# The opening of a one-core block program: order of the first roundings, two transfers for the first weights, and zero products on TensorE

## The chip, the cores and the metric

The program runs on one core of one Trainium2 chip, in one launch. The metric is the device time of that core in microseconds (us). The core has TensorE (PE in the profile; its weight loads are PEld), VectorE (DVE), ScalarE (ACT), GpSimd (POOL) and SyncE (SP), which here issues all the transfers, and 16 DMA engines that carry them.

## The reference, cut to what matters

The reference is two transformer blocks of two layers each over a sequence of 256 tokens and a width of 1024, in float32. The change touches only the first layer of the first block, up to its first few projections:

```python
def rmsnorm(x, g):
    xf = x.astype(jnp.float32)
    y = xf * lax.rsqrt(jnp.mean(xf * xf, axis=-1, keepdims=True) + RMS_EPS)
    return (y * g.astype(jnp.float32)).astype(x.dtype)

for l in range(DEPTH):
    h = rmsnorm(x, attn_norm[l])
    proj = h @ w_in[l]
    ...     # latent attention, gated convolution, pooling, windowed attention, output product
    x = x + mixed @ w_o[l]
    gate, up = jnp.split(rmsnorm(x, ffn_norm[l]) @ w_gate_up[l], 2, axis=-1)
    x = x + (jax.nn.silu(gate) * up) @ w_down[l]
```

The second block (state-space, recurrent and linear-attention mixers, and 32 experts per layer) follows and is not touched.

## The kernel before, in words

The activations x lie transposed in the core's memory: 128 partitions by 8 feature tiles by 256 tokens. The 16 output tiles of the first projection (1952 columns, 2048 with the repeated rotary ones) are computed one after another by `project(n)`. To keep float32 accuracy with the faster rounded format, every operand is split into a rounded high part and the rest: x times the norm's gain is rounded by ScalarE (`PreNorm.round`, L582) and the rest taken by VectorE (`PreNorm.rest`, L605); a weight tile is rounded by ScalarE (`Ring.round`, L505) and its rest taken by VectorE (`Ring.rest`, L511). `one_tile` then issues three products for each of 8 feature tiles, 24 per output tile (L630 to L632). The factor 1/rms is not in x: it is applied when a pair of projections leaves the accumulators (`evacuate`, L767), so the sum of squares can come later than the first products. ScalarE squares x in 8 instructions (`PreNorm.square`, L587), TensorE sums them over the partitions with a matrix of ones (`PreNorm.sum`, L613), and ScalarE makes 1/rms (`PreNorm.scale`, L593 and L596).

The weights of the first block come through a ring: `Ring.raw` has 4 slots, each with a unit of two weight tiles (1 MB); `high` and `low` have 4 places of one tile each. Four semaphore chains order it: SP issues the load of a unit into a slot once both tiles that were in it are split; ScalarE rounds tile n once its unit is loaded and tile n-4 has been used by TensorE; VectorE takes the rest after that; TensorE waits for the rest.

Nothing schedules the work at run time or when the program is built. Each engine has its own instruction stream in the order in which the functions for it are written in `stage_mix1`, and runs it strictly in that order; so a waiting instruction holds up all that stand behind it on its engine. In the first layer these are, before the change:

- SP (`load_first`): gains, x in two halves, unit 0, the matrix of ones, units 1 to 3, constants, the small weights of the attention (L720 to L722), then units 4 and on, each behind its slot's split.
- ScalarE: 8 tiles of x, weight tiles 0 to 3, 8 squares, 1/rms, weight tiles 4 to 8, then ln and exp for the latent norms (L956 to L961), weight tiles 9 and 10.
- VectorE: constants (`set_constants`, with a zeroed bank of 128x512 bfloat16 at L560), the rests of x, of weight tiles 0 to 4, pair 0 out, 5, 6, pair 1 out, and so on; behind the rest of weight tile 8 the scaling of the latent vectors (L840).
- TensorE: `project(0)`, the sum of squares, `project(1)` to `project(4)`, sums for the latent norms, `project(5)`, `project(6)`, then the query product (L1104), which waits for the scaled latent vectors.

`psX` is the last of the eight accumulator banks; the sum of squares goes there too, later.

Of the kernel before, what the change touches and what calls it, by code (L numbers as in the profile page):

```python
# [26 lines left out]
P = 128  # L27
D = 1024
S = 256
DT = D // P  # L30
# [288 lines left out]
class Stream:  # L319
# [28 lines left out]
    def round(self, act, i):  # L348

        act.wait_ge(self.loaded[i % self.slots], 16 * (i // self.slots + 1))  # L350
        if i >= self.n2:

            act.wait_ge(self.used, i - self.n2 + 1)
        for a, b in self.halves(i):
            act.activation(self.high[:, i % self.n2, a:b], self.raw[:, i % self.slots, a:b], ACT.Copy)\
                .then_inc(self.rounded, 1)

    def rest(self, dve, i):

        for n, (a, b) in enumerate(self.halves(i)):  # L360
            dve.wait_ge(self.rounded, 2 * i + n + 1)
            dve.tensor_tensor(self.low[:, i % self.n2, a:b], self.raw[:, i % self.slots, a:b],
                              self.high[:, i % self.n2, a:b], ALU.subtract).then_inc(self.split, 1)
# [83 lines left out]
W_HALF = DT * P  # L447
# [4 lines left out]
G_ORDER1 = (3, 2, 0, 1)  # L452
AHEAD = 4
LATE = 2


def ffn_order():
# [9 lines left out]
class Ring(Stage):  # L467
# [4 lines left out]
    def __init__(self, nc, dram):  # L472
        super().__init__(nc, "ring")
        self.dram = dram
        self.raw = self.sb("raw", [P, self.SLOTS, W_UNIT])
        self.high = self.sb("high", [P, AHEAD, W_HALF], F32R)
        self.low = self.sb("low", [P, AHEAD, W_HALF], F32R)
        self.loaded = [self.sem(f"loaded{i}") for i in range(self.SLOTS)]
        self.rounded = self.sem("rounded")
        self.split = self.sem("split")  # L480
        self.used = self.sem("used")
        self.issued = 0

    def load_while_split(self, sp, splits, most=N_ALL1):

        while 2 * self.issued < N_ALL1 and self.issued < most and \
# [4 lines left out]
            sp.dma_start(self.raw[:, g % self.SLOTS], self.dram[g]).then_inc(self.loaded[g % self.SLOTS], 16)  # L491
            self.issued += 1

    def raw_half(self, n):
        return self.raw[:, (n // 2) % self.SLOTS, (n % 2) * W_HALF:(n % 2 + 1) * W_HALF]

    def round(self, act, n):
        if n >= N_ALL1:
            return
        if n % 2 == 0:  # L500
            act.wait_ge(self.loaded[(n // 2) % self.SLOTS], 16 * (n // 2 // self.SLOTS + 1))
        if n >= AHEAD:

            act.wait_ge(self.used, n - AHEAD + 1)
        act.activation(self.high[:, n % AHEAD], self.raw_half(n), ACT.Copy).then_inc(self.rounded, 1)  # L505
# [33 lines left out]
def load_first(sp, k, f, ring, a):  # L539

    x = a["x_t"].rearrange("p (t s) -> p t s", t=DT)
    half = DT // 2
    sp.dma_start(f.vecs[:], a["vec1"].rearrange("l p n -> p l n")).then_inc(f.vec_loaded, 16)
    for i in range(2):
        sp.dma_start(k.x[:, half * i:half * (i + 1)], x[:, half * i:half * (i + 1)]).then_inc(f.x_loaded[i], 16)
    ring.load_while_split(sp, 0, 1)
    early = 2 * P
    sp.dma_start(k.const[:, 0:early], a["const"][:, 0:early]).then_inc(f.ones_loaded, 16)
    ring.load_while_split(sp, 0)
    sp.dma_start(f.const1[:], a["const"][:, N_KEPT:]).then_inc(f.const_loaded, 16)  # L550
    sp.dma_start(k.const[:, early:], a["const"][:, early:N_KEPT]).then_inc(f.const_loaded, 16)
    sp.dma_start(k.fin_g[:], a["fin_g"]).then_inc(k.gains_loaded, 16)
    sp.dma_start(k.ln[:], a["ln2"].rearrange("l p n -> p l n")).then_inc(k.gains_loaded, 16)
# [9 lines left out]
class PreNorm:  # L563
# [9 lines left out]
        self.ln_done = st.sem("ln_done")  # L573
        self.rstd_ready = st.sem("rstd_ready")

    def round(self, act):
        if self.first:
            act.wait_ge(self.f.vec_loaded, 16)
        for t in range(DT):
            if self.first and t % (DT // 2) == 0:  # L580
                act.wait_ge(self.f.x_loaded[t // (DT // 2)], 16)
            act.activation(self.f.high[:, t], self.k.x[:, t], ACT.Copy, scale=self.gain[:, t:t + 1])\  # L582
                .then_inc(self.rounded, 1)
# [11 lines left out]
        act.wait_ge(self.ln_done, 1)  # L595
        act.activation(self.f.rstd[:], self.f.lnv[:], ACT.Exp, scale=-0.5).then_inc(self.rstd_ready, 1)  # L596

    def rest(self, dve):
        if self.first:
            dve.wait_ge(self.f.vec_loaded, 16)  # L600
        for t in range(DT):
            if self.first and t % (DT // 2) == 0:
                dve.wait_ge(self.f.x_loaded[t // (DT // 2)], 16)
            dve.wait_ge(self.rounded, t + 1)
            dve.scalar_tensor_tensor(self.f.low[:, t], self.k.x[:, t], self.gain[:, t:t + 1], self.f.high[:, t],  # L605
                                     ALU.mult, ALU.subtract).then_inc(self.split, 1)
# [48 lines left out]
def stage_mix1(nc, k, f, ring, zero, L, a):  # L655
# [3 lines left out]
    with Stage(nc, f"mix{L}") as st:  # L659
        base = L * N_LAYER1  # L660
        first = L == 0
# [32 lines left out]
        norm = PreNorm(k, st, f, vecs[:, V1["attn_norm"][0]:], ps[:, 7], first)  # L694
# [12 lines left out]
        psX = ps[:, 7]  # L707
# [6 lines left out]
        with nc.Block() as block:  # L714

            @block.sync
            def _(sp):
# [4 lines left out]
                sp.dma_start(poolw[:], a["pool_w"][L].rearrange("p (k c) -> p k c", k=2)).then_inc(w_loaded, 16)  # L722
                ring.load_while_split(sp, base + N_MIX1 + AHEAD - LATE)

# [34 lines left out]
            def _(dve):  # L759
# [55 lines left out]

                if first:
                    set_constants(dve, k)
                norm.rest(dve)
                for n in range(0 if first else AHEAD - LATE, AHEAD):
                    ring.rest(dve, base + n)  # L820
                ring.rest(dve, base + 4)
                evacuate(0)
# [61 lines left out]
                group(3)  # L884
                for n in range(22, 28 - LATE):
                    ring.rest(dve, base + n)
# [9 lines left out]
            def _(act):  # L896
# [43 lines left out]

                if first:
                    act.preload_act_table_set("natural_log_exp_and_others")
                norm.round(act)
                if first:
                    for n in range(AHEAD):
                        ring.round(act, n)
                else:
                    act.preload_act_table_set("natural_log_exp_and_others")
                norm.square(act)
                if not first:  # L950
                    ring.round(act, base + AHEAD - 1)
                norm.scale(act)
                for n in range(4, 9):
# [54 lines left out]
            def _(pe):  # L1008
                def project(n):
                    ring.ready(pe, base + n)  # L1010
                    if n % 2 == 0 and n >= 4:

                        pe.wait_ge(evac, n // 2 - 1)
                    one_tile(pe, ps[:, (n // 2) % 2, (n % 2) * S:(n % 2 + 1) * S], ring.tiles(base + n), f,
                             norm.split if n == 0 else None).then_inc(ring.used, 1)
# [59 lines left out]
                def output(j):  # L1075
# [10 lines left out]
                            ins.then_inc(out_done, 1)  # L1086
                    ins.then_inc(ring.used, 1)

                project(0)
                norm.sum(pe)  # L1090
                for n in range(1, 5):
                    project(n)
                pe.wait_ge(latent_sq, 1)
                pe.wait_ge(norm.ln_done, 1)
# [14 lines left out]
                for blk in range(SB):  # L1109
                    ins = pe.matmul(ps[:, 6, blk * S:(blk + 1) * S], cn[:, 2, blk * P:(blk + 1) * P], wukv[:, 1],  # L1110
                                    start=True, stop=True)
# [23 lines left out]
                for g in range(4):  # L1135
                    rows, t = slice(64 * (g % 2), 64 * (g % 2) + 64), g // 2
# [25 lines left out]
def stage_ffn1(nc, k, f, ring, zero, L):  # L1162
# [3 lines left out]
    with Stage(nc, f"ffn{L}") as st:  # L1166
# [14 lines left out]
        with nc.Block() as block:  # L1181

            @block.sync
            def _(sp):
                ring.load_while_split(sp, base + len(order) + AHEAD - LATE)

            @block.vector
            def _(dve):
                ch = Chain(dve, dve_step)
                norm.rest(dve)  # L1190
                for n in range(AHEAD - LATE, AHEAD):
                    ring.rest(dve, base + n)
# [1980 lines left out]
```

## Time and profile before

| | us |
|---|---|
| runs before: median of 3 (lowest, highest) | 1953.72 (1951.14, 1955.69) |
| the profiled execution, its own time | 1956.74 |
| its span in the trace | 1955.0 |
| TensorE busy in the span | 1858.0 |
| VectorE, ScalarE busy | 832.1, 637.3 |
| granted TensorE clock, mean | 0.996 |

The span runs from the first to the last recorded instruction. "Busy" counts an engine's instructions, with the ends of matmuls modelled; the start-to-start distance of two matmuls tells more than their length. In a row of the timeline a group of like instructions is merged as "x8", and the bracket says how long the engine stood idle before it and which instruction or transfer released it. The granted clock is TensorE's as a share of full speed.

### The profile page before, as it was taken

Reading aid. Unit: us, or ns where it says so; the run is one execution under the profiler, and the core shown is the slowest. Engines: PE = TensorE matmul, PEld = TensorE weight load, DVE = VectorE, ACT = ScalarE, POOL = GpSimd, SP = SyncE. Lnnn points to the kernel's source line nnn. Section 1 sums busy time; section 2 is a strip of 40 time slices with the busy share of each in tenths; the row PEclk is TensorE's granted clock in tenths of the full one; section 3 lists DMA queues with packets and bytes.
Section 4 is the critical chain, followed back from the end, with each engine's and each line's share of the span. In section 5 each row is a group of like instructions: output and inputs, shape, how many; then the busy total and the mean of one; then the engine's idle time right before and its main releaser. Section 6 shows DMA issues by size and latency. Waiting matters only on the chain. (4 is left out here: it accounts for less than half of the span.)

```text
span 1955.0 us, 35987 instructions
## 1 busy us (share of the span) xinstructions
PE 1858.0 (95%) x15616; PEld 1266.6 (65%) x15626; DVE 832.1 (43%) x1687; ACT 637.3 (33%) x1209; POOL 52.2 (3%) x58
## 2 busy tenths in 40 slices
PE   7999999899999998899999999989899999999997
PEld 6889998789997887644444434378775444444443
DVE  5767777767775576411111111155734111111113
ACT  4565555565555342311111111143313111111112
POOL 0500000400000000000000000000000000000000
PEclk9999999999999999999999999999999999999999
DMA  7245554235552338499999999743395999999993
GB/s 287 96 147 191 192 194 169 87 131 193 191 176 70 98 99 342 177 407 426 427 427 427 427 427 426 309 124 110 127 380 192 428 427 427 426 426 427 427 426 164
DMA packets 54529, 540.18 MB, mean 276 GB/s; under 512 B 8640, under 2 KB 9568, under 8 KB 16736
## 3 DMA queue, kind: packets, MB, share of 16 engines
q1 hardware_dynamic: 54368, 537.83, 68.6%
q8 instruction: 126, 2.06, 0.4%
q14 instruction: 35, 0.29, 0.0%
HBM read 536.76 MB, written 1.05 MB: 275 GB/s over the span
## 5 line engine op out<-in xcount | busy, mean ns | idle before, releaser
L2971 PE MATMUL experts_psG<-places_gu,experts_xc 128*64 128x512 f32 x1344 | 297.8, 593 | 9.3 <-DMA places_gu<-in_moe_up 9.3
L511 DVE TENSOR_TENSOR ring_low<-ring_raw,ring_high 128x1024 fp32r<-128x1024 f32 x180 | 222.4, 1246 | 100.6 <-ACT ring_high L505 100.5
L2971 PEld LDWEIGHTS experts_psG<-places_gu,experts_xc 128*64 128x64 f32 x1344 | 96.8, 137 | 203.1 <-issue 184.3
L644 PE MATMUL ffn_ps<-first_x_split,ring_high 128*128 128x512 f32 x616 | 220.6, 396 | 0.3
L2898 DVE SCALAR_TENSOR_TENSOR experts_yc_low<-experts_psD,experts_slot_gate,experts_yc_high 128x512 fp32r<-128x512 f32 x64 | 48.1, 751 | 388.5 <-ACT experts_yc_high L2934 388.5
L505 ACT ACTIVATE ring_high<-ring_raw 128x1024 fp32r<-128x1024 f32 x180 | 186.8, 1051 | 70.5 <-PE ffn_ps L646 30.7
L645 PE MATMUL ffn_ps<-first_x_split,ring_low 128*128 128x256 f32 x704 | 183.4, 281 | 0.0
L2888 DVE TENSOR_TENSOR experts_sig<-experts_sig,experts_psG 128x256 f32<-128x256 f32 x64 | 27.0, 421 | 356.3 <-ACT experts_sig L2922 356.3
L2971 PE MATMUL experts_psG<-weights_gu,experts_xc 128*64 128x512 f32 x704 | 156.2, 593 | 5.1 <-DMA weights_gu<-in_moe_up 3.7
L2922 ACT ACTIVATE experts_sig<-experts_psG 128x256 f32<-128x256 f32 x64 | 24.6, 384 | 411.3 <-PE experts_psG L2971 411.3
L645 PEld LDWEIGHTS ffn_ps<-first_x_split,ring_low 128*128 128x128 f32 x704 | 132.1, 188 | 7.1
L644 PEld LDWEIGHTS ffn_ps<-first_x_split,ring_high 128*128 128x128 f32 x616 | 115.8, 188 | 24.9 <-issue 1.2
L2934 ACT ACTIVATE experts_yc_high<-experts_psD,experts_slot_gate 128x512 fp32r<-128x512 f32 x64 | 44.0, 687 | 262.9 <-PE experts_psD L3001 262.9
L2971 PEld LDWEIGHTS experts_psG<-weights_gu,experts_xc 128*64 128x64 f32 x704 | 50.0, 137 | 106.4 <-issue 95.0
L3001 PE MATMUL experts_psD<-places_d,experts_hT 128*64 128x512 f32 x512 | 116.9, 598 | 0.0
L2947 PE MATMUL experts_psX<-parts_selb,parts_x 128*128 128x64 bf16 x3072 | 99.8, 193 | 0.0
L622 PE MATMUL ffn_ps<-ffn_act_high,ring_low 128*128 128x256 f32 x352 | 98.6, 280 | 0.0
L621 PE MATMUL ffn_ps<-ffn_act_low,ring_high 128*128 128x256 f32 x352 | 98.3, 279 | 0.0
L620 PE MATMUL ffn_ps<-ffn_act_high,ring_high 128*128 128x256 f32 x352 | 98.3, 279 | 0.0
L2947 PEld LDWEIGHTS experts_psX<-parts_selb,parts_x 128*128 128x128 bf16 x3072 | 93.6, 98 | 0.5
L2001 PE MATMUL mixers_ps<-x_resid,mixers_w_raw 128*128 128x256 f32 x384 | 88.3, 386 | 4.5 <-ACT x_resid L233 2.2
L630 PE MATMUL mix_ps<-first_x_split,ring_high 128*128 128x256 f32 x256 | 76.6, 299 | 14.1 <-DVE ring_low L511 11.9
(531 smaller groups left out, 3243.4 us busy)
## 6 DMA issues: line engine op xcount, KB each, us to landing
ring_raw<-in_w SPq DMA_DIRECT2D x90, 1024.0 KB, 4.9
places_gu<-in_moe_gate SPq DMA_DIRECT2D x42, 2048.0 KB, 28.1
places_gu<-in_moe_up SPq DMA_DIRECT2D x42, 2048.0 KB, 29.6
places_d<-in_moe_down SPq DMA_DIRECT2D x32, 2048.0 KB, 26.0
weights_gu<-in_moe_up SPq DMA_DIRECT2D x22, 2048.0 KB, 28.0
weights_gu<-in_moe_gate SPq DMA_DIRECT2D x20, 2048.0 KB, 28.7
weights_d<-in_moe_down SPq DMA_DIRECT2D x16, 2048.0 KB, 26.0
experts_d_more<-in_moe_down SPq DMA_DIRECT2D x16, 2048.0 KB, 27.8
```

Source lines behind the costliest of these rows:

```text
L505: act.activation(self.high[:, n % AHEAD], self.raw_half(n), ACT.Copy).then_inc(self.rounded, 1)
L511: dve.tensor_tensor(self.low[:, n % AHEAD], self.raw_half(n), self.high[:, n % AHEAD], ALU.subtract)\
L620: pe.matmul(out, w[0][:, kk], high, start=False, stop=False)
L621: pe.matmul(out, w[0][:, kk], low, start=False, stop=False)
L622: return pe.matmul(out, w[1][:, kk], high, start=False, stop=stop)
L630: pe.matmul(out, w[0][:, kk], f.high[:, kk], start=kk == 0, stop=False)
L644: pe.matmul(out, w[0][:, kk], f.both[:, :, kk], start=kk == 0, stop=False)
L645: ins = pe.matmul(out[:, 0], w[1][:, kk], f.high[:, kk], start=False, stop=False)
L2001: return pe.matmul(out, a, c, start=kc == 0, stop=kc == DT - 1)
L2947: ins = pe.matmul(psX[:, t * SLOTS:(t + 1) * SLOTS], m.parts[:, i, blk, t * P:(t + 1) * P], selb[:, par, blk, 0:SLOTS], start=i == 0 and b ...
L2971: ins = pe.matmul(out, xc[:, kk], wgu[gu[0]][:, kk, :, j * S:(j + 1) * S], start=kk == 0, stop=kk == DT - 1)
L3001: ins = pe.matmul(psD[rows, :], hT[:, c, j * SLOTS:(j + 1) * SLOTS], wd[d[0]][:, 2 * j + c, i * 512:(i + 1) * 512], start=j == 0 and c == ...
```

## The change

SP now loads the first unit in two transfers of 512 KB, one per weight tile, and the first has a semaphore of its own. ScalarE rounds weight tile 0 between tiles 3 and 4 of x, and squares x right behind weight tile 1, ahead of weight tiles 2 and 3. VectorE takes the rests in the same order. TensorE first multiplies the zeroed bank by itself 24 times into `psX`, as soon as VectorE has set it, and sums the squares behind `project(1)`, where it stood behind `project(0)`. All of it is for the first layer alone; the other layers keep their order.

```diff
+ZEROS = 24
...
+    def load_first(self, sp):
+
+        for n, sem in enumerate((self.first_loaded, self.loaded[0])):
+            sp.dma_start(self.raw_half(n), self.dram[0, :, n * W_HALF:(n + 1) * W_HALF]).then_inc(sem, 16)
+        self.issued = 1
...
     def round(self, act, n):
         if n >= N_ALL1:
             return
-        if n % 2 == 0:
+        if n == 0:
+            act.wait_ge(self.first_loaded, 16)
+        elif n % 2 == 0 or n == 1:
             act.wait_ge(self.loaded[(n // 2) % self.SLOTS], 16 * (n // 2 // self.SLOTS + 1))
...
-    ring.load_while_split(sp, 0, 1)
+    ring.load_first(sp)
...
-    def round(self, act):
+    def round(self, act, tiles=range(DT)):
...
-        for t in range(DT):
+        for t in tiles:
...
-    def rest(self, dve):
+    def rest(self, dve, tiles=range(DT)):
...
-                norm.rest(dve)
-                for n in range(0 if first else AHEAD - LATE, AHEAD):
+                if first:
+                    norm.rest(dve, range(0, DT // 2))
+                    ring.rest(dve, 0)
+                    norm.rest(dve, range(DT // 2, DT))
+                    ring.rest(dve, 1)
+                else:
+                    norm.rest(dve)
+                for n in range(AHEAD - LATE, AHEAD):
                     ring.rest(dve, base + n)
...
-                norm.round(act)
                 if first:
-                    for n in range(AHEAD):
-                        ring.round(act, n)
+                    norm.round(act, range(0, DT // 2))
+                    ring.round(act, 0)
+                    norm.round(act, range(DT // 2, DT))
+                    ring.round(act, 1)
+                    norm.square(act)
+                    ring.round(act, 2)
+                    ring.round(act, 3)
                 else:
+                    norm.round(act)
                     act.preload_act_table_set("natural_log_exp_and_others")
-                norm.square(act)
-                if not first:
+                    norm.square(act)
                     ring.round(act, base + AHEAD - 1)
...
+                if first:
+                    pe.wait_ge(k.constants_set, 7)
+                    for _ in range(ZEROS):
+                        pe.matmul(psX, k.zero[:, 0:P], k.zero[:], start=True, stop=True)
                 project(0)
-                norm.sum(pe)
-                for n in range(1, 5):
+                if first:
+                    project(1)
+                    norm.sum(pe)
+                else:
+                    norm.sum(pe)
+                    project(1)
+                for n in range(2, 5):
                     project(n)
```

ScalarE, at the start of the first layer, before the change (`first_x_split` is the high part of x, `ring_high` that of a weight tile, `first_sq` the squares; `ring_loaded0` and `ring_loaded1` are the loads of units 0 and 1):

```order
L942 ACT_TABLE_LOAD
L582 ACTIVATE first_x_split<-x_resid,first_vecs 128x256 [waits first_x_loaded0,first_vec_loaded]
L582 ACTIVATE first_x_split<-x_resid,first_vecs 128x256 x3
L582 ACTIVATE first_x_split<-x_resid,first_vecs 128x256 [waits first_x_loaded1]
L582 ACTIVATE first_x_split<-x_resid,first_vecs 128x256 x3
L505 ACTIVATE ring_high<-ring_raw 128x1024 [waits ring_loaded0]
L505 ACTIVATE ring_high<-ring_raw 128x1024
L505 ACTIVATE ring_high<-ring_raw 128x1024 [waits ring_loaded1]
L505 ACTIVATE ring_high<-ring_raw 128x1024
L587 ACTIVATE first_sq<-x_resid 128x256 x8
```

The same engine and place after it (L582, L505 and L587 have become L592, L515 and L597):

```order
L958 ACT_TABLE_LOAD
L592 ACTIVATE first_x_split<-x_resid,first_vecs 128x256 [waits first_x_loaded0,first_vec_loaded]
L592 ACTIVATE first_x_split<-x_resid,first_vecs 128x256 x3
L515 ACTIVATE ring_high<-ring_raw 128x1024 [waits ring_first_loaded]
L592 ACTIVATE first_x_split<-x_resid,first_vecs 128x256 [waits first_x_loaded1,first_vec_loaded]
L592 ACTIVATE first_x_split<-x_resid,first_vecs 128x256 x3
L515 ACTIVATE ring_high<-ring_raw 128x1024 [waits ring_loaded0]
L597 ACTIVATE first_sq<-x_resid 128x256 x8
L515 ACTIVATE ring_high<-ring_raw 128x1024 [waits ring_loaded1]
L515 ACTIVATE ring_high<-ring_raw 128x1024
```

Weight tile 0 has moved ahead of four tiles of x and waits for its own half of unit 0; the squares have moved ahead of weight tiles 2 and 3.

TensorE, the first instructions of the first layer after the change; before it the stream began with the L640 row (then L630):

```order
L1112 MATMUL mix_ps<-zero_bank 128x512 [waits constants_set]
L1112 MATMUL mix_ps<-zero_bank 128x512 x23
L640 MATMUL mix_ps<-first_x_split,ring_high 128x256 [waits mix0_x_split,ring_split]
L641 MATMUL mix_ps<-first_x_split,ring_high 128x256
L642 MATMUL mix_ps<-first_x_split,ring_low 128x256
```

The 24 zero products stand ahead of `project(0)` and wait for the constants alone.

## Rows read from the trace of the kernel before

**Rows 1.** The page: span, and busy time of each engine.

```profile
span 1955.0 us, 35987 instructions
PE 1858.0 (95%) x15616; PEld 1266.6 (65%) x15626; DVE 832.1 (43%) x1687; ACT 637.3 (33%) x1209; POOL 52.2 (3%) x58
```

**Rows 2.** Windows: stretch, length, busy PE, PEld, DVE, ACT, POOL, clock, DMA share, GB/s.

```profile
0.00:50.00 50.00, 37.32 (x256) 34.72 (x258) 27.99 (x41) 24.35 (x38) 0.52 (x9) 1.00 0.73 281
900.00:950.00 50.00, 50.00 (x456) 23.14 (x454) 8.05 (x28) 9.14 (x24) 0.00 (x0) 1.00 1.01 426
```

**Rows 3.** PE's waits over the span: us in total, times, longest.

```profile
PE mix_ps L630 <- DVE ring_low L511: 11.9, 1, 11.9
PE experts_psG L2971 <- DMA places_gu<-in_moe_up: 9.3, 10, 1.9
```

**Rows 4.** Timeline of ACT: start, length, instruction, idle before and releaser.

```profile
5.64 3.30 ACT L582 ACTIVATE first_x_split<-x_resid,first_vecs 128x256 fp32r<-128x256 f32 x8 [3.65 <-DMA x_resid<-in_x_t]
9.53 2.00 ACT L505 ACTIVATE ring_high<-ring_raw 128x1024 fp32r<-128x1024 f32 x2 [0.59 <-DMA ring_raw<-in_w]
...
14.51 2.55 ACT L587 ACTIVATE first_sq<-x_resid 128x256 f32<-128x256 f32 x8
...
31.86 1.06 ACT L505 ACTIVATE ring_high<-ring_raw 128x1024 fp32r<-128x1024 f32 x1 [1.82 <-PE mix_ps L632]
33.09 0.47 ACT L956 ACTIVATE mix_g_lnv<-mix_ps,eps_sb 128x256 f32<-128x256 f32 x1 [0.18 <-PE mix_ps L1097]
```

**Rows 5.** Timeline of DVE.

```profile
1.00 0.27 DVE L560 MEMSET zero_bank<- 128x256 uint32 x1
6.29 3.25 DVE L605 SCALAR_TENSOR_TENSOR first_x_split<-x_resid,first_vecs,first_x_split 128x256 fp32r<-128x256 f32 x8 [5.02 <-ACT first_x_split L582]
10.61 2.36 DVE L511 TENSOR_TENSOR ring_low<-ring_raw,ring_high 128x1024 fp32r<-128x1024 f32 x2 [1.06 <-ACT ring_high L505]
...
35.12 1.27 DVE L840 SCALAR_TENSOR_TENSOR mix_cn<-mix_proj,first_vecs,mix_g_rstd 128x256 f32<-128x256 f32 x3
```

**Rows 6.** Timeline of PE.

```profile
11.89 0.58 PE L630 MATMUL mix_ps<-first_x_split,ring_high 128*128 128x256 f32 x1 [11.89 <-DVE ring_low L511]
...
16.48 0.28 PE L630 MATMUL mix_ps<-first_x_split,ring_high 128*128 128x256 f32 x1
...
16.84 3.61 PE L613 MATMUL mix_ps<-first_sq,const 128*128 128x256 f32 x16
20.10 0.47 PE L630 MATMUL mix_ps<-first_x_split,ring_high 128*128 128x256 f32 x1
...
23.12 0.28 PE L630 MATMUL mix_ps<-first_x_split,ring_high 128*128 128x256 f32 x1
...
38.54 3.62 PE L1104 MATMUL mix_ps<-mix_cn,mix_wuq 128*128 128x256 f32 x16
```

**Rows 7.** Timeline of SP's queue, stretches 0:60 and 14:14.7.

```profile
1.22 0.93 SPq L545 DMA_DIRECT2D x_resid<-in_x_t  x2
...
14.60 2.10 SPq L491 DMA_DIRECT2D ring_raw<-in_w  x1
```

**Rows 8.** DMA issues, stretches 2:3 and 14:15: KB, us to landing.

```profile
x_resid<-in_x_t SPq DMA_DIRECT2D x1, 512.0 KB, 5.2
...
ring_raw<-in_w SPq DMA_DIRECT2D x1, 1024.0 KB, 15.2
```

**Rows 9.** Windows round three long pauses of PE, columns as in rows 2.

```profile
308.90:311.30 2.40, 0.20 (x3) 0.08 (x1) 1.54 (x4) 1.23 (x4) 0.33 (x5) 1.00 0.61 227
...
619.00:621.40 2.40, 0.17 (x1) 0.03 (x1) 1.17 (x3) 1.54 (x4) 0.00 (x0) 1.00 0.00 0
...
1283.00:1285.00 2.00, 0.00 (x0) 0.00 (x0) 1.13 (x3) 1.34 (x4) 0.00 (x0) 1.00 0.01 4
...
1286.00:1288.00 2.00, 2.00 (x7) 1.58 (x6) 1.17 (x5) 1.98 (x6) 0.00 (x0) 0.54 0.00 0
```

**Rows 10.** Line 652, zero products of a later stage: count, shortest/median/longest ns, first and last start.

```profile
L652 PE MATMUL ffn_ps<-zero_bank x3: 377/378/378, 118.6 to 119.0; 128*128 128x512 bf16 x3
```

More of the change, by code:

```diff
@@ L478, in __init__ @@
         self.loaded = [self.sem(f"loaded{i}") for i in range(self.SLOTS)]
+        self.first_loaded = self.sem("first_loaded")
         self.rounded = self.sem("rounded")
@@ L596, in scale @@
         act.activation(self.f.rstd[:], self.f.lnv[:], ACT.Exp, scale=-0.5).then_inc(self.rstd_ready, 1)
-    def rest(self, dve):
+    def rest(self, dve, tiles=range(DT)):
         if self.first:
             dve.wait_ge(self.f.vec_loaded, 16)
-        for t in range(DT):
+        for t in tiles:
             if self.first and t % (DT // 2) == 0:
```

## The prediction

> **What bounds the kernel now.** I read the page first: TensorE is busy for 1858.0 of 1955.0 us [rows 1]. Then the windows: there are two kinds of stretch, the opening, in which TensorE is busy 37.3 of 50 us, and the expert stretches, in which the DMA engines run at 426 GB/s and TensorE is hardly ever idle [rows 2]. Then TensorE's waits: the largest single one of the whole program, 11.9 us, is its first, which ends with VectorE's rest of weight tile 0; the waits for expert weights are 9.3 us in ten pieces [rows 3]. So the program begins with a chain of transfers and roundings, and from 11.89 us on TensorE's queue sets the time. I then read the three timelines of the first 40 us side by side [rows 4 to 6].
>
> The opening chain before: x lands, ScalarE rounds its 8 tiles from 5.64 to 8.94, waits 0.59 us for unit 0 and rounds weight tile 0 from 9.53 on [rows 4]; VectorE takes its rest from 10.61 to about 11.83 (two rests of 1.22 in 2.36 us, [rows 5]); TensorE starts at 11.89 [rows 6]. Its first 21 products then take until 16.48, 0.22 us each, against 0.12 behind it: between the first products of tile 1 and tile 2 lie 24 products in 3.02 us, of which 0.19 is the change over from the sum [rows 6]. The granted clock column says 1.00 there, but the pace is that of the lower of the clock's two levels (256 columns in 0.213 us is 1.2 GHz; 0.107 would be 2.4). So project(0) lost 4.95 - 2.9 = about 2.05 us to a clock that rose only after 4.6 us of work behind an engine that had been idle from the start.
>
> **The change, part by part.**
>
> First transfer and new order of the roundings. The second half of x is issued at about 1.7 us (two issues in 0.93 from 1.22, [rows 7]) and lands 5.2 us later, at 6.9 [rows 8]; unit 0, twice its size, is there at 9.53 [rows 4]. The halves of unit 0 share these 2.6 us: the first lands half-way, at 8.2. I take 8.2; the ends are 8.0 and 8.6 (if the two halves' packets mix a good deal). ScalarE is free at 5.64 + 4 x 0.40 = 7.3, so it now waits 0.9 us for weights that come 1.3 us earlier. It rounds tile 0 from 8.2 to 9.25 (the pair of L505 takes 2.00 us, so 1.05 for one and 0.95 from start to start). VectorE takes the rest from 9.28 to 10.5, and TensorE can start at 10.57, **1.32 us earlier**.
>
> Will the rest of x be in time? ScalarE rounds tiles 4 to 7 from 9.15, one every 0.40, until 10.85; VectorE takes their rests behind the weights' rest, from 10.45, one every 0.40 (8 in 3.25 us, [rows 5]), so they are ready at 10.9, 11.3, 11.7 and 12.1. TensorE at full pace wants tile 4 at 10.57 + 4 x 0.36 = 12.0. No wait.
>
> Weight tile 1: ScalarE 10.75 to 11.8 (its half has landed at 9.5), VectorE 12.0 to 13.25, usable at 13.3. At full pace project(0) ends at 10.57 + 2.90 = 13.47. It fits by 0.15 us; an error here costs no more than itself.
>
> Zero products. VectorE has the zeroed bank at 1.27 [rows 5], so TensorE starts them at 1.33. Their pace in this trace, warm, is 0.21 us (length 0.378 us, three between 118.6 and 119.0, [rows 10]: 512 columns at 2.4 GHz); no row shows them at the lower level, for which I double it, 0.43. If the clock rises as it did before, 4.6 us after the first product, then 10.8 of the 24 are done at 5.9 us, and the other 13.2 take 2.8 us: the burst ends at 8.75. At the lower level throughout it would end at 1.33 + 24 x 0.427 = 11.6. The burst is hidden as long as it ends before 10.57. Behind it is a **new pause of 1.8 us** (8.75 to 10.57). What do such pauses do to the clock here? Three of 2.2 us are in the trace: behind those that end at 311.25 and 621.40 it stays at 1.00, behind the one that ends at 1285 it falls, to 0.54 from 1286 on [rows 9]. A shorter pause than all three, with dense work on both sides: I take it that the clock holds, about three times in four.
>
> The Trainium skill bears on this ("TensorE: Matmul & The Clock Gate", section "What's actually happening"): the default state is throttled, activity releases it, and the clock gate looks at how busy the array has been, not at what it multiplies. By that rule zeros serve as well as data; the trace of before agrees on the idle start and the slow first products, and has no burst of zeros long enough to show the rest. The sum by the rule is the one below. The same page lets the clock fall only after an idle window; the fall at 1286 follows a pause no longer than two that were harmless, so the rows, not the rule, set my one in four.
>
> With the clock up, project(0) takes 2.90 us in place of 4.95: the first product costs some 0.07 more and 24 x 0.118 = 2.83. **2.05 us gained.**
>
> Squares and their sum. project(1) runs 13.47 to 16.30. ScalarE squares from 11.7 to 14.3 (2.55 us, [rows 4]), and TensorE sums from 16.30, without a wait, 3.26 us (16.84 to 20.10, [rows 6]), to 19.56. The move itself saves nothing on TensorE; it keeps the sum from standing before squares that would not be ready (before, they ended at 17.06). Rounding tiles 2 and 3 now stands behind the squares: ScalarE 14.3 to 16.3, VectorE 15.3 to 17.9; tile 2 is ready at 16.6 and wanted at 19.75. Hidden. 1/rms comes at 20.8, tile 4 is rounded 20.7 to 21.8 and split at 23.0, wanted at 19.56 + 0.19 + 2 x 2.83 = 25.4. Hidden.
>
> So tile 2 starts at 19.56 + 0.19 = 19.75 where tile 2 stood at 23.12: **3.37 us in all** (1.32 + 2.05).
>
> Is it given back? The next landing that ScalarE meets is unit 4 (tiles 8 and 9): issued at 14.60 [rows 7], landed 15.2 us later, at 29.8 [rows 8], because all that SP issued before it goes first. Before, tile 8 was rounded at 31.86, released by TensorE; 3.37 earlier is 28.5. So there is a **new wait of 1.3 us on ScalarE**, up to 1.75 if the additional issue (0.43 us) shows in the landing. Queued behind it is the ln of the latent norms (before at 33.09, [rows 4]), which now starts at 30.8 to 31.25 and not at 29.7, and on VectorE the rest of tile 8 and the scaled latent vectors. These ended at 35.12 + 1.27 = 36.39 [rows 5]; I get 33.6 to 34.1. The query product that takes them started at 38.54 [rows 6], now 35.17. Slack 1.1 to 1.6 us, where there were 2.15. Hidden, at no cost. Later waits all hang on chains that move with TensorE, and the expert loads too are issued when buffers come free, not at a fixed time: the 3.4 us should reach the end.
>
> **The sum.** Against the profiled execution's own time: 1956.74 - 3.4 = 1953.3 us. That execution lies 3.0 us above the median of the runs, for no reason in the trace, so I give the forecast on the median's scale: 1953.72 - 3.4 = 1950.3 us. From above: if the half lands at 8.6, 0.4 less; if the clock rises late in other executions of before, up to about 0.6 more.
>
> **The rivals.**
>
> The clock falls in the pause, or in the first product's microseconds. For: the fall at 1286 [rows 9]; before, it stayed low for the first 4.6 us. Against: two of three pauses. Then project(0) loses up to 2.05 again, and at the latest starts as computed at 10.57: the gain is 1.3 to 1.7 us, 1952.2 us.
>
> Zeros do not raise the clock. No row here shows that they do. Then the burst ends at 11.6, project(0) starts at 11.65 at the low level and gains 0.25 us: 1953.5 us.
>
> The burst becomes the bound: **slower**. No row shows a long row of such products at the low level, each with its own weight load. If zeros do not raise the clock, and a weight load lay beside its product and not under the one before, a product would take 0.43 + 0.21 = 0.64 us and the burst 15.4 us. project(0) would start at 16.7, still at the low level, take its 4.95 us, and tile 2 would start at 16.7 + 4.95 + 2.83 + 3.26 + 0.19 = 27.9 against 23.12: 4.8 us slower, 1958.5 us. The point from which it decides is a mean zero product of (11.89 - 1.33) / 24 = 0.44 us with the clock low. Against: between 20.10 and 23.12 in rows 6 the weight loads lie under the products (24 in 3.02 us, 0.12 each behind the first), and 0.427 is just short of 0.44.
>
> The gain is given back at unit 4: for it the slack of 1.1 us must go, which takes a landing after about 31 us; a landing at 32 would cost 1 us, leaving 1951.3.
>
> **How the numbers follow.** Forecast 0.62; clock falls 0.20; zeros do not count 0.07; burst the bound 0.04; given back at unit 4, 0.07. The median of three runs that lie 4.5 us apart is itself uncertain by some 1.5 us, and this holds for both kernels, so a measured difference strays by about 2 us around each case. A difference of less than 0.2% (3.9 us) can't be told from none here. The forecast's 3.4 lies just inside it: of its 0.62, 0.28 falls beyond 3.9; the other gaining cases give 0.03 more, and 0.04 for falls of the clock at other pauses, whose place against the clock's own rhythm is shifted (each costs or spares some 1.7 us). Faster 0.35, same 0.59, slower 0.06. The range: 1950.3 with 3.4 to either side, taking in the falling clock and the zeros that don't count: 1946.8 to 1954.0. The forecast's own is 1947.8 to 1952.6.
>
> **What would show it.** L1112 x24 from 1.33 to about 8.8 with its pace halving on the way; L515 for tile 0 at 8.2; the first L640 at 10.6 and its pace 0.12 from the second product on; the sum (L623) at 16.3, the second project pair from 19.75; ScalarE waiting 1.3 us for a transfer at about 28.5; the query product at 35.2 without a wait. Wrong would be: products at 0.21 us after 10.6, a burst that ends after 10.6, or a query product released by VectorE.

## The result, and the profile after

The changed kernel takes 1963.26 us (median of 10 runs, 1957.69 to 1967.65), the kernel before, beside it, 1956.86 (10 runs, 1951.14 to 1958.91): a ratio of 1.0036, 95% interval 1.0023 to 1.0048. It is 6.4 us **slower** by the medians and 7.0 us by the ratio, where 3.4 us faster was forecast. The profiled execution took 1967.65 us, with a mean granted clock of 0.986 against 0.996; it is the slowest of the ten.

The page after, in answer to rows 1:

```profile
span 1965.9 us, 36035 instructions
PE 1876.3 (95%) x15640; PEld 1278.5 (65%) x15650; DVE 830.8 (42%) x1687; ACT 637.1 (32%) x1209; POOL 53.2 (3%) x58
```

48 instructions more, 24 products and 24 weight loads, and a span 10.9 us longer. The opening is not where it went. The timeline of PE after, in answer to rows 6:

```profile
1.33 6.78 PE L1112 MATMUL mix_ps<-zero_bank 128*128 128x512 bf16 x24 [1.33 <-DVE zero_bank L570]
10.57 0.38 PE L640 MATMUL mix_ps<-first_x_split,ring_high 128*128 128x256 f32 x1 [2.46 <-DVE ring_low L521]
...
17.85 3.62 PE L623 MATMUL mix_ps<-first_sq,const 128*128 128x256 f32 x16
21.11 0.47 PE L640 MATMUL mix_ps<-first_x_split,ring_high 128*128 128x256 f32 x1
...
36.73 3.61 PE L1133 MATMUL mix_ps<-mix_cn,mix_wuq 128*128 128x256 f32 x16
```

The first projection starts at 10.57, as worked out, and tile 2 at 21.11 where it stood at 23.12 [rows 6]: 2.0 us earlier, and the query product is 1.8 us earlier. The timeline of ACT after, in answer to rows 4, has the first half of the weights at 8.20 and the new wait for unit 4 (2.2 us, to 30.43), which stays hidden:

```profile
8.20 1.06 ACT L515 ACTIVATE ring_high<-ring_raw 128x1024 fp32r<-128x1024 f32 x1 [0.79 <-DMA ring_raw<-in_w]
...
30.43 1.06 ACT L515 ACTIVATE ring_high<-ring_raw 128x1024 fp32r<-128x1024 f32 x1 [2.21 <-DMA ring_raw<-in_w]
```

The loss is in the mixer stages, 670 us later. TensorE's waits over the whole span, first those of before that no transfer and no engine ends, then the same of after ("issue" is a wait for nothing that the profile shows, PEq the engine's own sequencer):

```profile
PE mixers_ps L239 <- PEq L2802: 2.8, 1, 2.8
...
PE mixers_ps L2004 <- issue: 1.0, 1, 1.0
...
PE mixers_ps L1876 <- issue: 0.5, 1, 0.5
```

```profile
PE mixers_ps L1905 <- issue: 4.1, 2, 2.4
...
PE mixers_ps L239 <- PEq L2831: 2.8, 1, 2.8
```

L1876 of before is L1905 of after: the end of a run of very small products (32x64), which TensorE takes at a great pace (73 of them in 0.81 us of work in the first window below, where a projection at 0.12 us a product has 7 in that time), and with them its instruction stream. Before, it stands still there once for 0.5 us; after, once in each of the two layers, 1.7 and 2.4 us. The other wait of before in these stages, 1.0 us in the second layer at L2004, the larger products right behind the small ones, is gone after; so the sum of both kinds went from 1.5 to 4.1 us, 2.6 more. The timeline of PE after shows the two places:

```profile
692.50 0.36 PE L1905 MATMUL mixers_ps<-mixers_tok 32*64 32x64 f32 x12 [1.69 <-issue]
```

```profile
1363.48 0.47 PE L1905 MATMUL mixers_ps<-mixers_tok 32*64 32x64 f32 x4 [2.44 <-issue]
```

And by each of them the clock falls: 1.2 us behind the end of the first wait, and in the last 0.7 us of the second. Windows of after, columns as in rows 2 (the clock is the number before the DMA share):

```profile
690.00:692.00 2.00, 0.81 (x73) 0.67 (x54) 0.72 (x1) 1.10 (x2) 0.00 (x0) 1.00 0.26 55
692.00:693.70 1.70, 1.20 (x19) 1.13 (x20) 0.75 (x1) 0.00 (x0) 0.00 (x0) 1.00 0.83 288
693.70:697.10 3.40, 3.40 (x18) 3.40 (x17) 2.96 (x4) 0.00 (x0) 0.00 (x0) 0.51 0.00 1
...
1361.00:1362.70 1.70, 0.04 (x3) 0.00 (x0) 0.00 (x0) 0.74 (x1) 0.00 (x0) 1.00 0.65 198
1362.70:1369.60 6.90, 6.12 (x40) 5.78 (x44) 3.72 (x4) 0.19 (x1) 0.00 (x0) 0.51 0.26 81
```

The trace of before has no low stretch at either place. So the working theory was: **the 48 added instructions move TensorE's instruction stream, and at its fastest place it now runs dry longer.** The page has 126 instruction packets of 2.06 MB together (16.3 KB each) on one queue, q8; the instruction bytes of both queues that carry instructions, 2.35 MB, over 35987 instructions make 65 bytes for one, so a packet holds about 250 (an estimate). That q8 carries TensorE's instructions shows in the pages of the experiments: it has 126 packets with 0, 48 or 128 instructions added to TensorE's stream, and 127 with 224 or 256. The rivals: the burst itself changes how the clock behaves later on, or the transfers and the new order do it.

### The profile page after: what moved, and what is told of

Read it like the earlier page. It is cut to its first block and busy times, and to the rows that moved or that the text cites. A ratio compares the mean times of both kernels' runs of the same rounds, so it can differ in the third digit from the quotient of the medians.

```text
span 1965.9 us, 36035 instructions
## 1 busy us (share of the span) xinstructions
PE 1876.3 (95%) x15640; PEld 1278.5 (65%) x15650; DVE 830.8 (42%) x1687; ACT 637.1 (32%) x1209; POOL 53.2 (3%) x58
## 3 DMA queue, kind: packets, MB, share of 16 engines
q8 instruction: 126, 2.06, 0.4%
HBM read 536.76 MB, written 1.05 MB: 274 GB/s over the span
## 5 line engine op out<-in xcount | busy, mean ns | idle before, releaser
L515 ACT ACTIVATE ring_high<-ring_raw 128x1024 fp32r<-128x1024 f32 x180 | 186.8, 1051 | 66.9 <-PE ffn_ps L656 30.9
L630 PE MATMUL ffn_ps<-ffn_act_high,ring_high 128*128 128x256 f32 x352 | 98.3, 279 | 0.0
L2030 PEld LDWEIGHTS mixers_ps<-x_resid,mixers_w_raw 128*128 128x128 f32 x384 | 74.2, 196 | 16.9 <-issue 6.5
```

What stands on the lines that cost most here:

```text
L630: pe.matmul(out, w[0][:, kk], high, start=False, stop=False)
L2030: return pe.matmul(out, a, c, start=kc == 0, stop=kc == DT - 1)
```

## The experiments

Each was timed beside the kernel before. In the table "added" is the number of instructions put into TensorE's stream ahead of the mixer stages, "dry" the sum of its waits for "issue" at the small products in the profiled execution, "behind" the same at the larger products right behind them (L2004 of before), "L239" the sum of the two waits at the starts of the norms behind the expert loops, "clock" the mean granted clock over the runs. e7 and e8 are one execution each: their waits can be read, their times can't be told from before's.

| kernel | added | us, median (runs) | before | ratio, 95% | dry | behind | L239 | clock |
|---|---|---|---|---|---|---|---|---|
| before | 0 | | | | 0.5 | 1.0 | 5.5 | 0.9946 |
| changed | 48 | 1963.26 (10) | 1956.86 | 1.0036 (1.0023 to 1.0048) | 4.1 | 0 | 5.5 | 0.9895 |
| e1 no zeros | 0 | 1953.34 (12) | 1957.26 | 0.9989 (0.9977 to 1.0) | 0.8 | 1.0 | 5.5 | 0.9947 |
| e2 zeros only | 48 | 1963.64 (6) | 1957.26 | 1.0038 (1.0025 to 1.0052) | 4.3 | 0 | 5.5 | 0.9900 |
| e3 24 tiny | 48 | 1963.99 (6) | 1957.26 | 1.0038 (1.0025 to 1.005) | 3.4 | 0 | 5.5 | 0.9915 |
| e11 24 tiny, layer 2 | 48 | 1963.29 (8) | 1955.54 | 1.0039 (1.0021 to 1.0057) | 3.0 | 0 | 5.5 | 0.9912 |
| e7 64 tiny | 128 | 1961.62 (1) | 1956.55 | | 4.1 | 0 | 5.5 | 0.995 |
| e8 112 tiny | 224 | 1957.50 (1) | 1956.55 | | 0 | 0.3 | 5.7 | 0.994 |
| e4 128 tiny | 256 | 1955.79 (11) | 1957.26 | 0.9996 (0.9987 to 1.0004) | 1.1 | 0.7 | 5.5 | 0.9958 |
| e5 change, 128 | 256 | 1953.71 (11) | 1956.55 | 0.9991 (0.9979 to 1.0004) | 0 | 1.0 | 5.6 | 0.9947 |
| e6 change, fuller | 256 | 1953.83 (11) | 1956.55 | 0.9987 (0.9976 to 0.9998) | 1.1 | 0.7 | 5.5 | 0.9945 |
| e12 change, head | 256 | 1955.18 (12) | 1957.16 | 0.9989 (0.9977 to 1.0001) | 0.8 | 0.7 | 5.5 | 0.9945 |
| e9 change, 112 | 224 | 1962.52 (12) | 1955.54 | 1.003 (1.0017 to 1.0043) | 0 | 0 | 12.1 | 0.9912 |
| e10 no burst, 112 | 224 | 1961.78 (10) | 1955.54 | 1.0032 (1.0014 to 1.005) | 0 | 0.7 | 12.1 | 0.9925 |

**e1, the change without its burst.**

```diff
-                    for _ in range(ZEROS):
-                        pe.matmul(psX, k.zero[:, 0:P], k.zero[:], start=True, stop=True)
```

> The changed kernel without its 24 zero products; transfers and the order of roundings stay. Stream theory (the 48 added TensorE instructions, 24 products and 24 weight loads, shift its instruction stream, so that it runs dry in the small products of the mixer stages: two waits of 1.7 and 2.4 us at L1905 where before had one of 0.5 us at L1876, and the clock falls behind both): 1.3 us faster than before, the wait at that line back at 0.5 us. Burst theory (the early burst changes how the clock behaves in all later pauses): the same time, but for another reason, about 1.3 us faster than before. Third theory (the transfers or the order of the roundings do it): still 6 to 7 us slower than before.

About 2 us faster than before by the ratio. The third theory falls: the transfers and the new order are not the loss.

**e2, the burst alone, on the kernel before.**

```diff
+                if first:
+                    pe.wait_ge(k.constants_set, 7)
+                    for _ in range(24):
+                        pe.matmul(psX, k.zero[:, 0:P], k.zero[:], start=True, stop=True)
                 project(0)
                 norm.sum(pe)
```

> The kernel before with nothing but the 24 zero products of 512 columns ahead of its first projection. Stream theory: the two waits at the small products are there, 3.6 us more than before, and two or three falls of the clock behind them at 1.7 us each, less 0 to 2 us from the warm first projection: 1962 us, 5 to 8 slower than before. Burst theory: also 5 to 8 us slower. Third theory: 0 to 2 us faster than before.

The whole loss is there (7.4 us by the ratio), with the dry waits of 4.3 us. Stream and burst theory both expected it. Together with e1 it takes the loss out of the transfers and the order and puts it on the 24 products.

**e3, as many instructions with next to no work.** The same edit with tiny products:

```diff
+                        pe.matmul(psX[0:32, 0:8], k.zero[:, 0:32], k.zero[:, 0:8], start=True, stop=True)
```

> The kernel before with 24 zero products of 8 columns and 32 weight columns in that place: as many instructions, almost no work for the clock to see, all of it in the first idle 11.9 us. Stream theory: 4 to 9 us slower than before, with the waits of about 2 us each at the small products. Burst theory: no change (within 1 us), and the wait of 0.5 us as before.

The 24 tiny products are over in 0.8 us, in the idle time before the first projection, which then starts at 11.91 (11.89 before); tile 2 starts 0.3 us earlier than before. The kernel is 7.4 us slower all the same. The burst theory falls here: it is the instructions, not their work.

**e11, the same 24 tiny products elsewhere**, under `if not first:` in place of `if first:`, so at the start of the second layer.

> The kernel before with the 24 tiny products of e3 not at its head but in the pause of 2.2 us at the start of the second layer: the opening is untouched, the mixer stages see the same shift of 48 instructions. Stream theory: as e3, two waits of 3.4 to 4.3 us together and 5 to 8 us slower than before. If something at the head is what counts: the time of before.

The same loss (7.6 us by the ratio), with the opening untouched; the waits are 3.0 us, a little under the 3.4 to 4.3 expected. What counts is that 48 instructions stand somewhere ahead of the mixer stages.

**e4, e7, e8: 128, 64 and 112 tiny products** in e3's place.

> The same with 128 tiny zero products, 256 instructions. The page has 126 instruction packets of 2.06 MB together, 16.3 KB each, and 2.35 MB for 35987 instructions, 65 bytes each, so a packet holds some 250. Stream theory, if it is the place of the packets' ends in the small products that counts: a shift by a whole packet puts them back, the wait is 0.5 us again and the time that of before (within 1 us). If it is only the number of added instructions that counts: slower than e3. Burst theory: no change.

> The kernel before with 64 tiny zero products, half a packet (128 instructions). One look: the wait at the small products in the trace. Stream theory with the place of the packets' ends: a value of its own, other than 0.5 (0 or 256 instructions) and 3.4 to 4.3 (48); if the wait only grew with the number added, over 4.3 us.

> The kernel before with 112 tiny zero products, 224 instructions, so 32 short of a packet. One look: the wait grew by about 3 us when the stream moved 48 on; moved 32 back it should vanish (0 us, from 0.5 to 1.1), if the place of the packets' ends decides; if not, no less than e4's 1.1 us.

256 added instructions cost nothing (0.9987 to 1.0004), 48 cost 7.4 us. At the small products 128 leave TensorE dry for 4.1 us and 224 not at all. So the loss does not grow with the number; at 256 the time is that of before again, which is what a packet of about 250 would do. Two expectations were met only in part: in e4 the wait at the small products is 1.1 and not 0.5 us, and the 4.1 us of e7 is not the value of its own that was expected but as much as with 48, the second of its two waits at another line (L1874). TensorE's waits at that place, in e7, e4 and e8 (in e8 the only one left there is at L2008):

```profile
PE mixers_ps L1874 <- issue: 2.3, 1, 2.3
...
PE mixers_ps L1880 <- issue: 1.8, 1, 1.8
```

```profile
PE mixers_ps L1880 <- issue: 1.1, 1, 1.1
```

```profile
PE mixers_ps L2008 <- issue: 0.3, 1, 0.3
```

The packets themselves can be seen in the DMA view, window by window of 0.2 us. Those of before and of after that bear on the first dry wait were on the queue at 688.2 to 688.4 and at 689.9 to 690.1:

```profile
q8 instruction: 1, 0.02, 27.5%
```

```profile
q8 instruction: 1, 0.02, 28.9%
```

TensorE went on at 690.75 and 692.50, so 2.5 us after the packet's window began in one and 2.6 in the other. The same distance holds in e3 (692.0 and 694.66), e4 (689.4 and 691.90), e7 (690.6 and 693.11), e8 (689.0 and 691.36) and in the second layer of after (1361.0 and 1363.48): 2.4 to 2.7 us in all seven. The reading that fits this, argued and not shown by itself: the packet comes when a certain place in the stream is reached, and the engine can use it some 2.5 us later; how long it stands dry depends on how much of the stream is left by then, and in a run of small products that is soon used up.

**e5 and e6, the whole change, moved on by a whole packet.** e5 has 28 tiny products ahead of the burst and 76 in the pause at the start of the second layer; e6 has 20 and 76, and 32 zero products in place of 24.

```diff
+                    for _ in range(28):
+                        pe.matmul(psX[0:32, 0:8], k.zero[:, 0:32], k.zero[:, 0:8], start=True, stop=True)
                     for _ in range(ZEROS):
                         pe.matmul(psX, k.zero[:, 0:P], k.zero[:], start=True, stop=True)
+                else:
+                    for _ in range(76):
+                        pe.matmul(psX[0:32, 0:8], k.zero[:, 0:32], k.zero[:, 0:8], start=True, stop=True)
```

> The whole change with 104 more tiny zero products (8 columns, 32 weight columns), 28 ahead of the burst and 76 in the pause of 2.2 us in which TensorE waits at the start of the second layer; with the 24 of the burst that is 128 products, 256 instructions, a whole instruction packet ahead of the mixer stages. Stream theory: the waits at the small products shrink from 4.1 us to 1.1 or less, and what the opening gained shows: 1.5 to 3 us faster than before, 8 us faster than the changed kernel. If the burst or the opening itself caused the loss: no faster than the changed kernel, 1963 us.

> The same with 32 products of 512 columns and 20 + 76 tiny ones, again 128: the burst now reaches to about 10.4 us (8 products at 0.427, 24 at 0.216, from 1.9), almost to the first projection. If the pause behind the burst is what let the clock fall at 11 us: no fall there, and up to 1.5 us faster than e5. If the clock falls whatever stands there: the same as e5, or 0.3 slower where the burst ends late.

Both take the whole loss away: by the ratios they are 1.8 and 2.5 us below before, so 8.8 and 9.6 us below the changed kernel. In e5 the burst ended 0.36 us before the first projection and the clock did not fall. The timeline of PE:

```profile
2.17 7.86 PE L1114 MATMUL mix_ps<-zero_bank 128*128 128x512 bf16 x24
10.39 0.39 PE L640 MATMUL mix_ps<-first_x_split,ring_high 128*128 128x256 f32 x1 [0.36 <-DVE ring_low L521]
...
19.41 0.47 PE L640 MATMUL mix_ps<-first_x_split,ring_high 128*128 128x256 f32 x1
```

Tile 2 at 19.41 is 3.7 us earlier than before, the forecast's 3.4 and a little. The tiny products in the second layer gave 0.8 of it back (they ran from 308.07 to 310.05 behind a start of 1.05 us, a pause of 3.0 us in place of 2.2). In e6 the burst held up the first projection, which started at 11.10 without a pause, and the clock did not fall; its median is the same.

**e9 and e10: 112 products**, to be rid of the last dry wait. e9 is e5 with 20 and 68 tiny ones; e10 is e1 with 112 at the head.

> The whole change with 88 tiny products (20 ahead of the burst, 68 in the pause at the start of the second layer), so 112 products in all, 32 instructions short of a packet. Stream theory: no wait at the small products, as in e8; 0.5 to 1 us better than e5 at the median, 3 us faster than before, near 1953.

> The change without its burst, with 112 tiny products in the burst's place: the earlier start of 1.3 us, no wait at the small products, and no work that could raise the clock before the first projection. Stream theory: about 2 us faster than before. If the warm first projection is worth anything at the median, e9 is 0.5 to 2 us faster than this; if the pause behind the burst gives it all back, the two are the same.

Both expectations failed. At the small products the dry wait is gone, as in e8, but another place pays: the first product of the norm behind each expert loop, L239, TensorE's waits in e9:

```profile
PE last_norm_n_ps L239 <- issue: 6.3, 1, 6.3
PE mixers_ps L239 <- issue: 5.8, 1, 5.8
```

5.5 us became 12.1. Between the expert loop and L239 stands a branch that skips code which these runs do not need. TensorE's branch, in e8 and then in e10 (shortest, median and longest of the two, in ns):

```profile
L3050 PEldq COMPARE_BRANCH  x2: 447/464/482, 1273.1 to 1937.8; - x2
```

```profile
L3075 PEldq COMPARE_BRANCH  x2: 3409/3660/3910, 1271.9 to 1940.9; - x2
```

In e8 an instruction packet was on the queue at 1269.4 to 1269.6, some 3.6 us before the branch; in e10 at 1272.8 to 1273.0, about 1 us after it had begun, and L239 went on 2.7 us after that window's start. So the stream theory was applied to one place too few: a jump waits for its packet too, and its distance to the packets' ends is another than that of the small products. Why the packets of e8 and e10, with the same 36221 instructions, lie differently against the branch stays open. e10 did not get its earlier start of 1.3 us either: its first projection started at 11.80, against 11.89 before.

**e12, the change with all 256 instructions at the head**: 112 tiny products, then 16 zero products.

> The whole change with its stream moved by one whole packet, all of it at the head: 112 tiny products (3.1 us by e4's pace) and then 16 of 512 columns in place of 24, 128 in all, so that the burst ends by 11.3 us at the latest and nothing stands in the second layer's pause, where e5 lost 0.8 us. Stream theory: waits at L239 as before (2.8 and 2.7), at the small products 1.1 or less; the opening gains 2 to 3.5 us; 1.5 to 3.5 us faster than before at the median. If the loss came from the opening: 1961 or more.

2.2 us faster than before by the ratio, no better than e1, e5 or e6. In the profiled execution the first half of the weights came at 9.43, not at 8.20, and the first projection started at 11.80. The timeline of ACT, and q8 between 7.2 and 7.4:

```profile
9.43 1.06 ACT L515 ACTIVATE ring_high<-ring_raw 128x1024 fp32r<-128x1024 f32 x1 [2.32 <-DMA ring_raw<-in_w]
```

```profile
q8 instruction: 1, 0.02, 29.0%
```

The padding at the head did that, or goes with it every time. In the four kernels with 112 or 128 tiny products there the first weights came late (e10 and e12: 9.43, against 8.02 to 8.62 in after, e1, e5, e6 and e9; e8 and e4, with the unit in one transfer: 10.88 and 10.84, against 9.47 to 9.63 in before, e2, e3, e7 and e11). In those four alone an instruction packet was on q8 between 7.2 and 7.8; the others have none from 2 to 15 us. That the packet itself delays the weights is argued from this, not shown. No version stands clear of the others: e1, e5, e6 and e12 lie at 0.9987 to 0.9991, and only for e6 does the interval end below 1.

## Why the prediction was wrong

- **The start of the opening: right.** First half at 8.20 (8.2 forecast), rests and first projection at 10.57 (10.57). With the same transfers and at most 28 tiny products at the head the landing lay between 8.02 and 8.62 in five executions, as good as the 8.0 to 8.6 of the forecast.
- **The burst: right in kind.** It ended at 8.11 (8.75 forecast): 23 distances of 0.427 or 0.216 us in 6.4 us make 7 slow ones, so the clock rose 2.9 us into it and not 4.6. Zeros do raise the clock.
- **The pause behind it: the rival came true.** The forecast had the clock hold three times in four. It fell at 11.05 in after, behind a pause of 2.46 us, and at 11.55 in e2, behind 3.49; it held in e12, behind 2.51, in e9, behind 1.24, and in e5, behind 0.36. Part of the miss is the length of the pause: the burst ended early, so 1.8 us became 2.46. Windows of after:

```profile
9.00:11.00 2.00, 0.43 (x3) 0.43 (x4) 1.71 (x3) 2.00 (x6) 0.00 (x0) 1.00 1.02 393
11.00:12.00 1.00, 1.00 (x7) 1.00 (x6) 1.00 (x3) 1.00 (x2) 0.00 (x0) 0.54 1.03 434
12.00:14.00 2.00, 2.00 (x12) 2.00 (x11) 1.23 (x2) 2.00 (x8) 0.00 (x0) 0.50 1.00 422
```

 So the opening gained 2.0 us instead of 3.4; the rival said 1.3 to 1.7. That by itself is a smaller gain, not a loss.
- **Unit 4: right in kind.** The unit landed at 30.43 (29.8 forecast) and the new wait was 2.2 us (1.3 to 1.75 forecast); the scaled latent vectors ended at 34.8 and the query product took them at 36.7.
- **The step that failed: "Later waits all hang on chains that move with TensorE [...] the 3.4 us should reach the end."** This takes the program behind the opening for a rigid body that moves as a whole. The 24 products were weighed by their time, hidden, and their 48 instructions not at all. They moved the stream against its packets. In the profiled pair the waits at and right behind the small products grew by 2.6 us (4.1 against 1.5), and by the two long ones lie 10.2 us at the low clock (3.4 and 6.8) that before did not have.
- **The size.** From the mean clocks of the runs, (1 - clock) x 2 x 1960 is an estimate of the time spent at the low level: 41 us after, 21 before, 33 in e3. In e3, whose opening is nearly that of before, 7.4 us of loss are then 1.9 of waiting (3.4 against 1.5) and 5.5 from 12 us more at the low clock, 0.46 us for each; at half the pace 0.5 is the most that one can cost. Of after's 20 us more, 3.4 lie in the opening and are counted in its gain of 2.0; the other 16.6 cost 7.6 at the same price, and 7.6 + 2.6 - 2.0 = 8.2, where 7.0 was measured. The waits here are those of one execution and the clocks carry three digits, so the split into waiting and clock is good to a microsecond or two. That the added instructions cause both together is shown by e3, e11, e4 and e5.
- **The base.** The forecast of 1950.3 stands on a median of three runs, 1953.72; that of ten was 1956.86, and the profiled execution of 1956.74, taken to lie 3.0 us high, was a usual one. So 3.1 of the 13 us between 1950.3 and 1963.26 are the base, and no mechanism.

Do the clock's falls come *from* the dry waits? Ten such waits of 1.4 us or more are in the traces, two in each of the five kernels with 48 or 128 added instructions. By nine of them the clock fell, at the earliest 0.7 us before the wait's end and at the latest 1.3 behind it; the second of e11, 1.61 us, left it at 1.00. In the nine other kernels no stretch of 685 to 705 or of 1350 to 1375 is at the low clock. Windows by the first wait in e2, e3, e11 and e7:

```profile
694.20:697.60 3.40, 3.40 (x18) 3.40 (x17) 2.88 (x4) 0.00 (x0) 0.00 (x0) 0.50 0.02 5
```

```profile
694.90:698.30 3.40, 3.40 (x27) 3.35 (x16) 3.17 (x4) 0.00 (x0) 0.00 (x0) 0.50 0.22 84
```

```profile
695.10:698.50 3.40, 3.40 (x18) 3.40 (x18) 3.21 (x4) 0.00 (x0) 0.00 (x0) 0.50 0.17 62
```

```profile
693.50:696.90 3.40, 3.40 (x47) 3.28 (x33) 2.68 (x4) 0.00 (x0) 0.00 (x0) 0.50 0.33 128
```

So these falls go with the waits; a wait of that length was not made in another way. They are not all of the clock's part. Summed over windows of 1 us, the profiled execution of after has 53 us at the low level and that of before 19, and of the 34 more only 10.2 lie by the waits and 3.4 in the opening; the rest is elsewhere (3.4 us each from 618.6, 741.5 and 1874.7, for example), and why stays open. In one execution the mean clock does not tell the kernels apart: e7, with both waits and both falls, has 0.995. Over the runs it does: 0.9895 to 0.9925 in every kernel with long waits that was timed more than once, 0.9945 to 0.9958 in every one without.

## What to carry to other kernels

An edit to a long unrolled program adds instructions as well as work: look in the waits for "issue" and sequencer waits far behind the edit, and compare them before anything else when a time moves with no cause at the edit. Where such a wait appears, pad the stream where the engine is idle anyway (here with tiny products, to a whole packet's worth), and time more than one padding, since each place has its own. A long padding at the head went with first weights 0.8 to 1.4 us later here, so look at the first landings too. A burst that warms the clock should reach to the work that it is for: behind pauses of about 2.5 us its effect was lost once and kept once, behind 3.5 us lost, behind 1.2 and 0.4 us kept, in one execution each. What the warm start is worth at the median is not shown: e1, which has no burst, is as fast as e5, e6 and e12.

## What the runs showed of the hardware

- TensorE goes on 2.4 to 2.7 us after the start of the 0.2 us window in which its instruction packet was carried, in all seven cases looked at; with some 250 instructions to a packet, a shift of 48 instructions cost 7 us of 1957 and one of 256 nothing.
- A branch of TensorE's that is 0.4 to 0.5 us long in e8 took 3.4 and 3.9 us in e10, where its packet came after it had begun.
- Dry waits of 1.4 to 2.6 us went with a fall of the clock nine times out of ten.
- 128 products of 8 columns with 32 weight columns took 3.6 us in e4, 0.028 us each; in after a burst of 24 with 512 columns, all of zeros, took 6.8 us, the low level for its first 2.9 us included.
- With 112 tiny products at the head (e10 and e12) an instruction packet was carried between 7.2 and 7.4 us, and the first half transfer of 512 KB landed at 9.43 us, against 8.02 to 8.62 in the five kernels with 28 or fewer.
